# Where a two-layer hybrid encoder works off the conditioning weights of its first layer

## The chip, the cores and the metric

One core of one Trainium2 chip runs the whole program. The time is that of the device, from launch to end, in microseconds (us); lower is better. The engines are TensorE (PE; its weight loads are the row PEld), VectorE (DVE), ScalarE (ACT), GpSimd (POOL) and SyncE (SP), which here issues the loads.

## The reference

Two layers over x of 256 tokens by 1024 channels, float32. Each layer draws six vectors (shift, scale and gate, twice) from a conditioning vector c:

```python
c_act = jax.nn.silu(c)
for layer in range(DEPTH):
    ada = c_act @ ada_w[layer] + ada_b[layer]          # 1024 x 6144
    sh1, sc1, gt1, sh2, sc2, gt2 = jnp.split(ada, 6, axis=-1)
    h = modulate(rmsnorm(x, norm_mix_w[layer]), sh1, sc1)
    x = x + gt1[:, None, :] * token_mixer(h, positions, ...)
    h = modulate(rmsnorm(x, norm_ffn_w[layer]), sh2, sc2)
    f = swiglu(h, ...) if layer % 2 == 0 else moe_swiglu(h, ...)
    x = x + gt2[:, None, :] * f
return rmsnorm(x, final_norm_w)
```

The token mixer projects h to the inputs of a gated DeltaNet branch (short convolution, chunked delta rule with a triangular inverse per 64 tokens, then a scan over four chunks) and of a sliding-window attention branch, gates and merges both, and projects once more. The channel mixer is a dense SwiGLU (width 3584) in layer 0 and the top 2 of 8 experts in layer 1.

## The kernel before

**Units.** All weights come as units of 1 MB (128 partitions by 2048 float32) into a ring of six slots. The list `units`, written out by hand at the top, is the order of their loads and also the order in which VectorE takes them. SyncE issues the load of unit u once unit u - 6 is taken (`load`). Most units are split for TensorE: ScalarE copies them to `w_hi` in a rounded format, VectorE subtracts to get `w_lo` (`take`), and TensorE makes three products of high and low parts. Three pairs of `w_hi` and `w_lo` rotate. In ScalarE's and VectorE's programs `ahead(key, by)` works off all units up to that key and `by` split units more; `product` does that and then waits until TensorE has used the unit.

**Conditioning units.** `("ada", l, q, kh)` is half kh of the rows of 512 of the 6144 columns of `ada_w`; q runs from 0 to 11. They aren't split. VectorE adds four slices of 128x512, each times a column of silu(c), into `ada_acc` (L1687, L1689), and when both halves are in, TensorE sums over the partitions with small products against a column of ones, `ada_piece` (L1064), into four columns of a PSUM bank. `ada_columns` adds the bias. A third accumulation may not begin before TensorE has read the first of its buffer, so VectorE waits there for `ada_ps`. Of layer 0, q 0 to 3 (shift and scale of the mixer) are needed before its first projection, q 4 and 5 (its gate) and q 6 to 9 (shift and scale of the channel mixer) at the end of the token mixer, and q 10 and 11 (the last gate) only at the end of the channel mixer, where `gate_diag` and `gate_row` turn them into a row over all partitions.

**Order of layer 0's token mixer** (the same code runs for layer 1, without conditioning units, since those of layer 1 stand in layer 0's channel mixer). Split units: qkvz 0 to 5, swq 0 and 1, swkv, qkvz 6 and 7, gate 0 to 7, wb 0 and 1, wa 0 and 1, four mix. TensorE runs the projections, the attention, the intra-chunk products (last at L1295 on), half of gate 0, the first transposes of the inverse, then five levels of the inverse (`for lev in range(1, 6)`): products of L1321, the block of gate `lev`, products of L1345 and L1347. VectorE masks and subtracts between these, and takes gate `lev + 1` in between. Then come the scan over four chunks (from L1400) with pieces of gates 6 and 7 between its products, wb 0 and 1, wa 0 and 1, and the mix projection. wa needs `oa_lo`, which VectorE makes after it has read wb 0 and taken wa 0.

Conditioning units stand in the ring: three after qkvz 7, seven between the gates (taken ahead of level 1 and in levels 1 to 4: one, then 1, 1, 2, 2), two after each wb unit and two after wa 0. VectorE takes the first three at two `take_upto` calls between the softmax and the inverse. `ada_piece` stands after gate 0, in levels 1, 3, 4 and 5, after wb 0, after wb 1 and after wa 0.

**Layer 0's channel mixer** has 14 steps of fg, fu and the previous step's fd (`for i in range(2 * FC)`); two conditioning units of layer 1 and one `ada_piece` go with each of the steps 0 to 11. The router's slot numbers are made in bank 2 at step 1.

## Time and profile before

| | |
|---|---|
| median of 3 runs | 1880.84 us (1880.74 to 1880.88) |
| the profiled execution | 1880.96 us |
| its span, first to last instruction | 1879.2 us |
| TensorE busy | 96% of the span, granted clock 0.986 |
| VectorE busy | 80% |
| ScalarE busy | 56% |
| layer 0 token mixer | about 43 to 336 us |
| layer 0 channel mixer | about 336 to 601 us |
| layer 1 token mixer | about 601 to 866 us |
| experts | the rest |

Three kinds of rows are used. A row of the page gives an engine's busy time, share and number of instructions. A row of the timeline gives start and length in us, engine, line, operation, tiles, count, and in brackets how long the engine had been idle and what released it. A row of a stretch gives start:end and length, then busy time (and instructions) of PE, PEld, DVE, ACT and POOL, then the granted TensorE clock (1.00 is 2.4 GHz, 0.50 is 1.2 GHz), the mean share of the DMA engines, and GB/s. The ends of the stretches in layer 0's mixer are the starts of TensorE's instructions: 42.87 the first projection, 121.27 the attention's transposes, 153.69 the end of the intra-chunk products, 165.20 level 1 (L1321), 182.46, 194.32, 207.97 and 221.62 the gate blocks of levels 2 to 4 and what follows them, 232.76 the scan (L1400), 287.17 wa 0, 303.85 the mix projection. In layer 1 they are 601.16, 677.23, 709.63, 718.83, 732.97, 744.83, 756.69, 768.55, 778.86, 827.47 and 842.06. The step numbers of the channel mixer count from 0.

### The profile page before, as it was taken

The numbers are of one execution on the slowest core, as the hardware profiler recorded it, in microseconds if no ns is written. First come the engines' busy times: TensorE is split into PE (matmuls) and PEld (weight loads), VectorE is DVE, ScalarE is ACT, GpSimd is POOL, SyncE is SP. The second block draws the span as 40 slices with busy tenths as digits, with TensorE's granted clock in tenths as the row PEclk, the third lists the DMA queues.
The fourth block names the chain that finished last, engine by engine and source line by source line (L and its number), as shares of the span: only waits on it lengthen the run. The fifth ranks groups of instructions, "written<-read, shape, count | busy, mean of one in ns | idle before, by whom it ended". The sixth has DMA issues, their size and how long they took to land.

```text
span 1879.2 us, 26149 instructions
## 1 busy us (share of the span) xinstructions
PE 1799.1 (96%) x10008; PEld 1527.8 (81%) x10014; DVE 1498.2 (80%) x1449; ACT 1060.3 (56%) x903; POOL 72.2 (4%) x133
## 2 busy tenths in 40 slices
PE   6988999899999999989999999999999999999997
PEld 6878887899997879987778888888888888888875
DVE  6768748977765757456998898888988899888898
ACT  2453233433333462245667777777777777777765
POOL 4010000000000010000000001000000000000100
PEclk9999998999999999999999999999999999999999
DMA  8625636798873513235999999999999999999994
GB/s 299 197 90 181 200 113 224 244 318 297 281 261 108 161 58 106 74 113 179 345 335 367 387 352 387 371 358 389 359 375 369 363 390 359 368 383 353 388 392 172
DMA packets 261446, 519.94 MB, mean 277 GB/s; under 512 B 12170, under 2 KB 75892, under 8 KB 261364
## 3 DMA queue, kind: packets, MB, share of 16 engines
q1 hardware_dynamic: 257988, 506.21, 76.2%
q0 software_dynamic: 3376, 12.58, 1.7%
q8 instruction: 58, 0.95, 0.2%
q14 instruction: 24, 0.20, 0.0%
HBM read 510.90 MB, written 7.86 MB: 276 GB/s over the span
## 4 chain that ended last, share of the span: by engine, by line
PE 81%; DVE 13%; ACT 3%; issue 2%; DMA 1%; SPq 0%; DVEq 0%; ACTq 0%
PE bank L1043 18%; PE bank L1045 18%; PE bank L1044 18%; PE bank L1049 6%; PE bank L1051 5%; PE bank L1050 5%; DVE w_lo L1671 2%; DVE ada_acc L1689 2%; DVE w_lo L1791 1%; PE bank L1605 1%; ACT w_hi L729 1%; PE bank L1064 1%; PE bank L1347 1%; ACT w_hi L954 1%; DMA xs<-in_x_dram 1%
## 5 line engine op out<-in xcount | busy, mean ns | idle before, releaser
L1791 DVE TENSOR_TENSOR w_lo<-ring,w_hi 128x2048 fp32r<-128x2048 f32 x336 | 767.1, 2290 | 96.1 <-ACT w_hi L954 92.0
L954 ACT CAST w_hi<-ring 128x2048 fp32r<-128x2048 f32 x336 | 642.4, 1912 | 132.4 <-PE bank L1045 129.1
L1043 PE MATMUL bank<-w_hi,xg_hi 128*128 128x512 f32 x896 | 357.2, 399 | 0.7 <-DVE w_lo L1791 0.7
L1044 PE MATMUL bank<-w_lo,xg_hi 128*128 128x512 f32 x896 | 352.9, 394 | 0.0
L1045 PE MATMUL bank<-w_hi,xg_lo 128*128 128x512 f32 x896 | 352.9, 394 | 0.0
L1671 DVE TENSOR_TENSOR w_lo<-ring,w_hi 128x2048 fp32r<-128x2048 f32 x96 | 219.6, 2291 | 99.1 <-ACT w_hi L729 98.5
L1049 PE MATMUL bank<-hT_hi,w_hi 128*128 128x256 f32 x912 | 265.5, 291 | 12.1 <-DVE w_lo L1671 8.1
L1050 PE MATMUL bank<-hT_lo,w_hi 128*128 128x256 f32 x912 | 258.4, 283 | 0.0
L1051 PE MATMUL bank<-hT_hi,w_lo 128*128 128x256 f32 x912 | 258.3, 283 | 0.0
L729 ACT CAST w_hi<-ring 128x2048 fp32r<-128x2048 f32 x96 | 182.3, 1903 | 79.6 <-PE bank L1045 42.1
L1043 PEld LDWEIGHTS bank<-w_hi,xg_hi 128*128 128x128 f32 x896 | 168.1, 188 | 42.7 <-issue 2.7
L1045 PEld LDWEIGHTS bank<-w_hi,xg_lo 128*128 128x128 f32 x896 | 168.0, 188 | 40.5
L1044 PEld LDWEIGHTS bank<-w_lo,xg_hi 128*128 128x128 f32 x896 | 168.1, 188 | 38.1
L1049 PEld LDWEIGHTS bank<-hT_hi,w_hi 128*128 128x128 f32 x912 | 174.9, 192 | 18.4 <-issue 7.8
L1043 PE MATMUL bank<-w_hi,h_hi 128*128 128x512 f32 x448 | 180.8, 404 | 0.0
L1050 PEld LDWEIGHTS bank<-hT_lo,w_hi 128*128 128x128 f32 x912 | 175.3, 192 | 1.5 <-issue 1.4
L1045 PE MATMUL bank<-w_hi,h_lo 128*128 128x512 f32 x448 | 176.2, 393 | 0.0
L1044 PE MATMUL bank<-w_lo,h_hi 128*128 128x512 f32 x448 | 175.7, 392 | 0.0
L1051 PEld LDWEIGHTS bank<-hT_hi,w_lo 128*128 128x128 f32 x912 | 175.2, 192 | 0.0
L1689 DVE SCALAR_TENSOR_TENSOR ada_acc<-ring,c_silu,ada_acc 128x512 f32<-128x512 f32 x160 | 120.2, 751 | 5.7
L1045 PEld LDWEIGHTS bank<-w_hi,h_lo 128*128 128x128 f32 x448 | 84.0, 188 | 20.1
L1044 PEld LDWEIGHTS bank<-w_lo,h_hi 128*128 128x128 f32 x448 | 84.3, 188 | 17.6
(417 smaller groups left out, 2158.7 us busy)
## 6 DMA issues: line engine op xcount, KB each, us to landing
ring<-in_moe_w_gate_dram SPq DMA_DIRECT2D x112, 1024.0 KB, 7.3
ring<-in_moe_w_up_dram SPq DMA_DIRECT2D x112, 1024.0 KB, 7.5
ring<-in_moe_w_down_dram SPq DMA_DIRECT2D x112, 1024.0 KB, 7.3
ring<-in_ada_w_dram SPq DMA_DIRECT2D x48, 1024.0 KB, 5.5
ring<-in_w_in_dram SPq DMA_DIRECT2D x38, 1024.0 KB, 5.2
ring<-in_ffn_w_gate_dram SPq DMA_DIRECT2D x14, 1024.0 KB, 7.0
ring<-in_ffn_w_up_dram SPq DMA_DIRECT2D x14, 1024.0 KB, 5.1
ring<-in_ffn_w_down_dram SPq DMA_DIRECT2D x14, 1024.0 KB, 6.5
```

The costliest lines, as they stand in the source:

```text
L729: act.copy(w_hi[buf][:], ring[:, ring_slot, :]).then_inc(hi_ready, 1)
L954: act.copy(w_hi[MOE_BUF[p % NS_MOE]][:], ring[:, p % RING, :]).then_inc(hi_ready, 1)
L1043: pe.matmul(o, xh, wh, start=start, stop=False)
L1044: pe.matmul(o, xh, wl, start=False, stop=False)
L1045: return pe.matmul(o, xl, wh, start=False, stop=stop)
L1049: pe.matmul(o, wh, xh, start=start, stop=False)
L1050: pe.matmul(o, wh, xl, start=False, stop=False)
L1051: return pe.matmul(o, wl, xh, start=False, stop=stop)
L1064: ins = pe.matmul(ps[bank][:, 4 * q + c:4 * q + c + 1], ada_acc[:, (NQ * l + q) % 2, c * P:(c + 1) * P], ones[:, 0:1], start=not begun, st ...
L1671: dve.tensor_tensor(w_lo[buf_of[s]][:], ring[:, u % RING, :], f32(w_hi[buf_of[s]][:]), ALU.subtract).then_inc(taken, 1)
L1689: ins = dve.scalar_tensor_tensor(acc, w[:, kk, :], ck, acc, ALU.mult, ALU.add)
L1791: dve.tensor_tensor(w_lo[b][:], ring[:, p % RING, :], f32(w_hi[b][:]), ALU.subtract).then_inc(taken, 1)
```

## The change

Of layer 0's sixteen conditioning units q 4 to 11, twelve stay in the token mixer and four (q 10, 11) move to steps 0 and 1 of the channel mixer; layer 1's then stand in steps 2 to 13. In the ring, q 4 goes between swq 1 and swkv, the first half of q 5 between swkv and qkvz 6, one unit after each of the gates 1 to 5, q 8 after gate 7, and q 9 after wa 0. VectorE's two extra `take_upto` calls go. `ada_piece` stands after gate 0 as before, then in levels 2 and 4, after wb 0, after wb 1 and after wa 1. In the channel mixer the columns of q 10 and 11 go to bank 2, so the router's slot numbers there move by 128 columns; the gate diagonal is made at step 2 instead of 12, layer 1's columns are read after the last step, and the gate row uses bank 0 instead of 3, with a wait for the last SiLU. The warming matmuls at the start of layer 1 write to bank 1.

```diff
--- before.py
+++ after.py
@@ -72,19 +72,19 @@
             units.append((("qkvz", l, j), True))
         for kh in range(2):
             units.append((("swq", l, kh), True))
+        if l == 0:
+            ada_units(2)
         units.append((("swkv", l), True))
+        if l == 0:
+            ada_units(1)
         for j in (6, 7):
             units.append((("qkvz", l, j), True))
-        if l == 0:
-            ada_units(3)
         for j in range(8):
             units.append((("gate", l, j), True))
             if l == 0:
-                ada_units((1, 1, 1, 2, 2, 0, 0, 0)[j])
+                ada_units((0, 1, 1, 1, 1, 1, 0, 2)[j])
         for cc in range(2):
             units.append((("wb", l, cc), True))
-            if l == 0:
-                ada_units(2)
         for cc in range(2):
             units.append((("wa", l, cc), True))
             if l == 0 and cc == 0:
@@ -94,7 +94,7 @@
                 units.append((("mix", l, cc, kh), True))
 
     mixer_units(0)
-    ada1 = [("ada", 1, q, kh) for q in range(NQ) for kh in range(2)]
+    ada1 = ada0 + [("ada", 1, q, kh) for q in range(NQ) for kh in range(2)]
     for i in range(2 * FC):
         units.append((("fg", i), True))
         if ada1:
@@ -1152,7 +1152,7 @@
                             turn_x(0, m_xn)
                         ada_piece(0, q, 0, True)
                 else:
-                    warm(24, 0)
+                    warm(24, 1)
                     turn_x(2 * l, m_xn)
                 def narrow(w, bank):
 
@@ -1323,8 +1323,8 @@
                         ins.then_inc(u_ps, 1)
                     pe.wait_ge(gate_s, 8 * l + lev)
                     two_blocks(("gate", l, lev), 0)
-                    if l == 0 and lev != 2:
-                        ada_piece(0, {1: 5, 3: 6, 4: 7, 5: 8}[lev], 1)
+                    if l == 0 and lev in (2, 4):
+                        ada_piece(0, 4 + lev // 2, 1)
                     if lev == 5:
 
                         pe.wait_ge(kgb_s, l + 1)
@@ -1434,19 +1434,19 @@
                 pe.wait_ge(gate_s, 8 * (l + 1))
                 half_branch("wb", 0, (2, 3), ob_hi, ob_lo, 1)
                 if l == 0:
-                    ada_piece(0, 9, 1)
+                    ada_piece(0, 7, 1)
                 half_branch("wb", 1, (0, 5), ob_hi, ob_lo, 0)
                 pe.wait_ge(ln2_s, 2 * (l + 1))
                 half_branch("wb", 1, (0, 5), ob_hi, ob_lo, 1)
                 if l == 0:
-                    ada_piece(0, 10, 1)
+                    ada_piece(0, 8, 1)
                 pe.wait_ge(oa_s, l + 1)
                 branch("wa", 0, (6, 7), oa_hi, oa_lo)
-                if l == 0:
-                    ada_piece(0, 11, 1)
                 half_branch("wa", 1, (4, 5), oa_hi, oa_lo, 0)
                 pe.wait_ge(yb_s, 4 * l + 2)
                 half_branch("wa", 1, (4, 5), oa_hi, oa_lo, 1)
+                if l == 0:
+                    ada_piece(0, 9, 1)
                 for kh in range(2):
                     pe.wait_ge(y_s, 2 * l + kh + 1)
                     for cc in range(2):
@@ -1493,14 +1493,17 @@
                         two_blocks(("fu", i), 1)
                         if i:
                             f_down(i - 1)
-                        if i < NQ:
-                            ada_piece(1, i, 3)
+                        if i < 2:
+                            ada_piece(0, NQ - 2 + i, 2)
+                        else:
+                            ada_piece(1, i - 2, 3)
                         if i == 1:
                             pe.wait_ge(upper_s, 1)
-                            pe.matmul(ps[2][:, 0:P], ones[:], upper[:], start=True, stop=True)
-                            pe.matmul(ps[2][:, P:P + 2], upper[:], ones[:, 0:2], start=True,
+                            pe.matmul(ps[2][:, P:2 * P], ones[:], upper[:], start=True, stop=True)
+                            pe.matmul(ps[2][:, 2 * P:2 * P + 2], upper[:], ones[:, 0:2], start=True,
                                       stop=True).then_inc(logit_ps, 1)
-                    gate_row(2, f_dg, (2, 3))
+                    pe.wait_ge(fs_s, 2 * FC)
+                    gate_row(2, f_dg, (2, 0))
                     f_down(2 * FC - 1)
 
 
@@ -1908,11 +1911,7 @@
                     dve.tensor_tensor(KB[:, :, here], kT[:, :, here], beta, ALU.mult)
                     dve.tensor_tensor(vT[:, :, here], vT[:, :, here], beta, ALU.mult).then_inc(kb_s, 1)
                 divide(1)
-                if l == 0:
-                    take_upto(u_of[("ada", 0, 4, 0)])
                 out_low(0)
-                if l == 0:
-                    take_upto(u_of[("ada", 0, 5, 0)])
 
                 dve.wait_ge(exps_s, 6 * l + 6)
                 link(dve.tensor_tensor(XT, X, wide(before_blk[:], [P, TB * H, P], 1), ALU.mult))
@@ -2024,7 +2023,7 @@
                     dve.tensor_tensor(hT_lo[:, half, :], y_sum[:, half, :], f32(hT_hi[:, half, :]),
                                       ALU.subtract).then_inc(y_s, 1)
                 if l == 0:
-                    ada_columns(0, 1, NQA, NQ)
+                    ada_columns(0, 1, NQA, NQ - 2)
                     dve.wait_ge(ada_s, 2)
                 gate_diag(2 * l + 1, l, 2, m_dg)
                 ahead(("mix", l, 1, 1), 0)
@@ -2074,18 +2073,19 @@
                         dve.tensor_tensor(f_lo[i % 2][:], f_h[:], f32(f_hi[i % 2][:]), ALU.subtract).then_inc(fhl_s, 1)
                         if i == 2:
                             dve.wait_ge(logit_ps, 1)
-                            dve.tensor_copy(slots[:], ps[2][:, 0:P])
+                            dve.tensor_copy(slots[:], ps[2][:, P:2 * P])
                             for tb in range(TB):
-                                dve.tensor_scalar(tok_c[:, tb, 0:1], ps[2][:, P:P + 1], float(tb * P), None, ALU.add)
-                            dve.tensor_scalar(spare, ps[2][:, P:P + 1], float(2 * T), None, ALU.add)
-                            dve.tensor_scalar(spare_n, ps[2][:, P:P + 1], -1.0, -float(2 * T), ALU.mult, ALU.add)
-                            link(dve.tensor_scalar(rsm[:, 0, :], ps[2][:, 0:E], -1.0, float(E), ALU.mult, ALU.add))
-                        if i == NQ:
-                            ada_columns(1, 3, 0, NQ)
+                                dve.tensor_scalar(tok_c[:, tb, 0:1], ps[2][:, 2 * P:2 * P + 1], float(tb * P), None, ALU.add)
+                            dve.tensor_scalar(spare, ps[2][:, 2 * P:2 * P + 1], float(2 * T), None, ALU.add)
+                            dve.tensor_scalar(spare_n, ps[2][:, 2 * P:2 * P + 1], -1.0, -float(2 * T), ALU.mult, ALU.add)
+                            link(dve.tensor_scalar(rsm[:, 0, :], ps[2][:, P:P + E], -1.0, float(E), ALU.mult, ALU.add))
+                            ada_columns(0, 2, NQ - 2, NQ)
                             dve.wait_ge(ada_s, 3)
                             gate_diag(2, 0, 5, f_dg[:])
+                    ada_columns(1, 3, 0, NQ)
+                    dve.wait_ge(ada_s, 4)
                     ahead(("fd", 2 * FC - 1), 0)
-                    gate_copy(2, f_gt, (2, 3))
+                    gate_copy(2, f_gt, (2, 0))
                     for tb in range(TB):
                         if tb == 0:
                             dve.wait_ge(first_ps, 2)
```

## Rows read from the trace of the kernel before

**Rows 1.** The page: busy time of each engine.
```profile
PE 1799.1 (96%) x10008; PEld 1527.8 (81%) x10014; DVE 1498.2 (80%) x1449; ACT 1060.3 (56%) x903; POOL 72.2 (4%) x133
```

**Rows 2.** Stretches of layer 0's mixer: start:end, length, each engine's busy time, clock.
```profile
42.87:121.27 78.40, 74.90 (x506) 67.59 (x507) 50.00 (x90) 40.11 (x48) 4.95 (x6) 0.98 0.58 188
...
153.69:165.20 11.51, 9.06 (x66) 9.05 (x65) 10.61 (x14) 0.89 (x3) 0.00 (x0) 0.85 0.37 120
165.20:182.46 17.26, 14.29 (x123) 13.94 (x122) 13.52 (x16) 4.16 (x3) 0.00 (x0) 1.00 0.71 243
182.46:194.32 11.86, 11.37 (x99) 11.18 (x98) 10.20 (x13) 2.38 (x2) 0.00 (x0) 1.00 0.55 178
194.32:207.97 13.65, 12.52 (x107) 12.14 (x106) 12.77 (x16) 2.39 (x2) 0.00 (x0) 1.00 0.68 194
...
221.62:232.76 11.14, 10.37 (x91) 10.18 (x89) 4.27 (x4) 4.43 (x6) 0.00 (x0) 1.00 0.50 141
232.76:287.17 54.41, 48.40 (x351) 43.76 (x352) 30.29 (x38) 17.95 (x21) 0.00 (x0) 0.94 0.39 128
287.17:303.85 16.68, 15.63 (x105) 15.54 (x106) 14.77 (x16) 2.94 (x2) 0.00 (x0) 0.79 0.86 304
```

**Rows 3.** The same stretches in layer 1's mixer, cut at the same instructions.
```profile
601.16:677.23 76.07, 72.58 (x507) 65.24 (x507) 47.90 (x78) 39.90 (x46) 4.95 (x6) 0.98 0.44 139
...
709.63:718.83 9.20, 6.88 (x56) 6.68 (x56) 8.97 (x13) 0.96 (x3) 0.00 (x0) 1.00 0.37 114
718.83:732.97 14.14, 13.41 (x112) 13.06 (x113) 8.72 (x9) 4.08 (x3) 0.00 (x0) 1.00 0.58 149
732.97:744.83 11.86, 11.38 (x99) 11.19 (x98) 7.29 (x9) 2.38 (x2) 0.00 (x0) 1.00 0.39 90
...
768.55:778.86 10.31, 9.53 (x84) 9.34 (x82) 4.27 (x4) 4.28 (x6) 0.00 (x0) 1.00 0.30 102
778.86:827.47 48.61, 43.95 (x335) 39.68 (x335) 19.06 (x22) 17.87 (x21) 0.00 (x0) 0.99 0.20 66
827.47:842.06 14.59, 14.29 (x96) 14.09 (x96) 9.25 (x9) 3.17 (x3) 0.00 (x0) 0.79 0.47 146
```

**Rows 4.** VectorE in order of time: one pair of conditioning units and the next split.
```profile
265.76 0.49 DVE L1687 TENSOR_SCALAR ada_acc<-ring,c_silu 128x512 f32<-128x512 f32 x1 [0.56 <-ACT work L899]
...
271.74 2.29 DVE L1671 TENSOR_TENSOR w_lo<-ring,w_hi 128x2048 fp32r<-128x2048 f32 x1
```

**Rows 5.** VectorE and then TensorE in order of time, around swkv in layer 0.
```profile
93.64 4.50 DVE L1671 TENSOR_TENSOR w_lo<-ring,w_hi 128x2048 fp32r<-128x2048 f32 x2 [2.50 <-ACT w_hi L729]
106.25 2.29 DVE L1671 TENSOR_TENSOR w_lo<-ring,w_hi 128x2048 fp32r<-128x2048 f32 x1 [8.11 <-ACT w_hi L729]
...
103.60 0.69 PE L1043 MATMUL bank<-w_hi,hT_hi 128*128 128x256 f32 x1
```

**Rows 6.** Layer 1's mixer: VectorE in order of time, and a wait of TensorE.
```profile
740.79 0.69 DVE L1963 TENSOR_TENSOR work<-work,bank 128x512 f32<-128x512 f32 x1 [3.42 <-PE bank L1347]
...
809.01 2.29 DVE L1671 TENSOR_TENSOR w_lo<-ring,w_hi 128x2048 fp32r<-128x2048 f32 x1 [8.12 <-ACT w_hi L729]
...
828.53 2.28 DVE L1671 TENSOR_TENSOR w_lo<-ring,w_hi 128x2048 fp32r<-128x2048 f32 x1
...
PE bank L1049 <- DVE oa_lo L2012: 4.5, 1, 4.5
```

**Rows 7.** Two stretches at the start of the channel mixer, columns as in rows 2.
```profile
342.22:344.87 2.65, 0.00 (x0) 0.00 (x0) 2.65 (x3) 2.62 (x4) 0.00 (x0) 1.00 0.42 70
345.40:348.80 3.40, 3.40 (x18) 3.40 (x18) 3.29 (x5) 1.04 (x1) 0.00 (x0) 0.50 1.04 389
```

**Rows 8.** Channel mixer steps 11 and 12 as stretches; VectorE in step 3.
```profile
531.24:549.10 17.86, 17.86 (x129) 16.75 (x128) 12.64 (x10) 6.73 (x5) 0.00 (x0) 1.00 0.84 295
549.91:566.95 17.04, 17.04 (x122) 15.95 (x122) 9.21 (x7) 6.17 (x5) 0.00 (x0) 1.00 0.60 186
...
397.71 2.29 DVE L1671 TENSOR_TENSOR w_lo<-ring,w_hi 128x2048 fp32r<-128x2048 f32 x1 [1.79 <-ACT w_hi L729]
```

## The prediction

> **What bounds the kernel now.** I read the page first: TensorE is busy 96% of the span, VectorE 80% [rows 1], so as a whole the kernel is a TensorE kernel, and only a stretch in which TensorE waits or runs slowly can give anything back. A "unit" here is one 1 MB piece of weights; conditioning units are worked off by VectorE alone (four multiply-adds of 128x512), all others are split by ScalarE and VectorE for TensorE. The two token mixers are the same code; only the first carries conditioning units: 16 in its ring order. So I cut both mixers at the same TensorE instructions and laid the lengths side by side [rows 2, 3]. That is the view that decides. The query/key/value part differs by 2.3 us (78.40 and 76.07), all of it in the first matmuls, ahead of what the change touches. From the end of the intra-chunk products on, layer 0 is longer by 2.31 us (start of the inverse), 3.12, 0, 1.79, 1.79 and 0.83 (levels 1 to 5), 5.80 (scan to the start of the last branch) and 2.09 (last branch): 17.7 us in all, the most that conditioning can cost there. Level 2, with one unit and no column product, costs nothing: 11.86 in both layers, as in levels 3 and 4 of layer 1 (level 4 of layer 0 is like its level 3). So a unit costs nothing while VectorE has idle time in front of what it must deliver; in levels 3 and 4, with two units each, it has not.
>
> **Prices.** A pair of units takes VectorE 271.74 - 265.76 = 5.98 us, about 2.9 and 3.1 for its halves [rows 4]. The column product that TensorE makes of each finished pair costs 11.14 - 10.31 = 0.83 us (level 5, the only difference there [rows 2, 3]).
>
> **The change part by part,** in order of time. My model of layer 0 after is layer 1 before plus the units and products that it still has.
>
> 1. Three units go ahead of the key/value weights: two between the last query unit and "swkv", one behind it. VectorE splits the last query unit and swkv back to back, 4.50 us from 93.64, so the second starts near 95.85 [rows 5]. With the pair between, swkv's low part is ready at 95.85 + 5.98 + 2.29 = 104.12. TensorE wants it at 103.60 [rows 5]. What is queued behind: VectorE's next split, which has 8.11 us of idle time before it [rows 5] and takes the third unit for nothing, and ScalarE's copies of swkv's result, on which the whole normalisation chain hangs, so the delay is not absorbed. Cost +0.56 (0.5 to 1.0). The weights behind are loaded three places later in the six-slot ring: the load of qkvz 7 is issued when swq 1 is taken, near 95.9, and its split comes after that of 106.25, over 10 us later, against 3.6 us of transfer for 1 MB at 295 GB/s [rows 8]; it hides.
>
> 2. The three units between softmax and the inverse vanish. Layer 0 goes from 11.51 to layer 1's 9.20 [rows 2, 3]; its one column product (unchanged, q 4) falls into the wait for VectorE that layer 1 has there. I take 9.27: -2.24. Much of that is clock: it was 0.85 here against 1.00 in layer 1 [rows 2, 3], which is half speed for 0.3 x 11.51 = 3.45 us and costs up to half of that, 1.7. If the clock falls all the same, the gain is only 0.5.
>
> 3. Levels 1 to 5 carry 1, 1, 1, 1, 1 units instead of 1, 1, 2, 2, 0, the one ahead of level 1 goes, and products come at levels 2 and 4 instead of 1, 3, 4 and 5. The least idle time of VectorE in a layer 1 level is 3.42 us [rows 6] against at most 3.1 for a unit, so all five hide, by 0.3 us or more. Level 1: 17.26 to 14.14, -3.12. Level 2: 11.86 to 11.86 + 0.83, +0.83. Level 3: 13.65 to 11.86, -1.79. Level 4: 13.65 to 12.69, -0.96. Level 5: 11.14 to 10.31, -0.83. Sum -5.87. Were the 0.3 us not there, each level would lose up to 0.5.
>
> 4. The last pair of the scan (q 8) stands before the first branch weights: VectorE is idle 8.12 us there in layer 1 [rows 6], enough for 5.98. The pairs that stood ahead of the second "wb" unit, the first "wa" unit and so on (6 us each, in front of oa_lo, for which TensorE waits) go. In layer 1 TensorE still waits 4.5 us for oa_lo [rows 6], and the products of q 7 and q 8 (1.7 us) fall into that. So 54.41 becomes 48.61: -5.80 (the largest term).
>
> 5. Last branch. The pair q 9 now stands before the second "wa" unit. In layer 1's times its split runs at 828.53 [rows 6]; with the pair, it is ready at 828.53 + 5.98 + 2.29 = 836.8, 9.3 us after the branch begins at 827.47. Then the second half unit takes TensorE 5.8 us at full clock and the product 0.8: 15.9 after 16.68 before. But half of such a unit falls in a slow stretch in both layers (granted clock 0.79 [rows 2, 3]), and the wait ahead of the unit invites another, worth up to 1.7 us (half of 3.4). I take 17.3: +0.6, with -0.8 and +1.0 as ends. Output projection and norm are unchanged; what is late next there is TensorE itself.
>
> 6. Channel mixer. The four units stand where two of layer 1's pairs stood, and everything shifts by two steps; only steps 12 and 13 gain load. The gate diagonal and a column copy move on VectorE from step 12 to step 2: a pass over half the elements of a split (half of 2.25 [rows 5]) and a copy of 8 columns, some 1.4 us, within its 1.79 us of idle time before the next split that waits [rows 8]. DMA share rises in step 12 from 0.60 towards 0.84, as in step 11, where TensorE was busy 17.86 of 17.86 us [rows 8]. What does cost is TensorE: two more products in a stretch where it never rests: +1.66. The extra wait before the gate row (the SiLU of the last step) is long met, one f_down earlier; the bank numbers cost nothing.
>
> **Sum:** +0.56 - 2.24 - 5.87 - 5.80 + 0.6 + 1.66 = -11.1 us. The profiled execution was 1880.96 us (span 1879.2), the median of the runs 1880.84, so I apply it to the median as it stands: 1880.84 - 11.1 = 1869.7.
>
> **The clock, trace against page.** TensorE waited 2.65 us at 342.22 and the granted clock then stood at 0.50 (1.2 GHz) for 3.4 us [rows 7]. The Trainium skill (TensorE: Matmul & The Clock Gate, "HAM oscillation") lets only idle gaps longer than this one re-throttle the array; the trace disagrees. By the page, the shorter gaps of part 2 could never have lowered the clock, and its 1.7 us would not be there to gain: the sum would be 9.4. By the row a wait of such a length can bring half speed behind it. Everything after layer 0's mixer shifts by some 11 us, so that slow stretches of layer 1 may come or go, up to 1.7 us each.
>
> **Rivals.**
> A. *Half the gain.* VectorE's chain is not what sets the inverse, scan and branch; with the units gone ScalarE or the clock holds the same events, so the middle of the stages keeps. Priced as parts 2, 4 and 5 at half: -1.1 - 5.87 - 2.9 + 1.0 + 0.56 + 1.66 = -6.7, 1874.2. Against it: layer 1 runs the same chain in the short time on the same engines. Chance 0.13.
> B. *More.* Part 5 keeps the clock (-0.8 instead of +0.6) and two of layer 1's slow stretches vanish. Half speed for 3.4 us holds 18 matmuls [rows 7]; at full speed step 12 ran 122 in 17.04, 24 in that time [rows 8]: 0.9 us lost, at most 1.7, so 1.3 each: -11.1 - 1.4 - 2.6 = -15.1, 1865.7. Chance 0.13.
> C. *Slower: the load queue.* The channel mixer is the stretch with the highest DMA share, 0.84 [rows 8]. If the 4 MB moved there can't be hidden, they cost their transfer, 4.2 MB at 295 GB/s = 14.2 us, against 11.1 gained plus nothing: +3.1, 1884. It decides once less than 3 us of these transfers find room. Against it: step 12 moved 186 GB/s for 17.04 us, so room for two more units is there [rows 8]. Chance 0.02.
> D. *The change does little:* pair q 4 ahead of swkv is late by its load, and the chain of part 1 loses what the inverse gains: within 0.2% (3.8 us). It needs swkv some 8 us late, where my sum has it half a microsecond late. Chance 0.02.
>
> **How the numbers follow.** The forecast holds with 0.70 (1867.5 to 1872). The 80% range takes in the forecast, B and the near part of A: 1865.5 to 1873.5. A measurement of this kernel can tell about 0.2% (3.8 us) from no change; forecast, B and most of A are beyond it: faster 0.95, same 0.03, slower 0.02.
>
> **What would show it.** In the changed trace: swkv's first matmul waits about half a microsecond for w_lo; the inverse start takes 9.3 us at granted clock 1.00; the levels take 14.1, 12.7, 11.9, 12.7, 10.3; the scan stage 48.6 with TensorE still waiting near 3 us for oa_lo; TensorE waits for w_lo before the second wa unit; channel mixer steps 12 and 13 at 17.9 us each. Wrong would be: a level over 13 us, a wait on a DMA in the channel mixer, or an oa_lo wait over 4 us.

## The result, and the profile after

The changed kernel takes 1867.24 us (median) against 1880.74 for the kernel before in the same session: a ratio of 0.9928 [0.9908, 0.9947], 13.5 us less. One of its five executions is slow (2629.68 us at a granted clock of 0.628); the other four took 1862.07 to 1870.31 us, with a median of 1865.9. The profiled one took 1867.24 us, with a span of 1865.5. Measured twice more, on two other chips, its median was 1866.91 and 1867.41 (ratios 0.9933 and 0.9941, below).

On the page of the changed kernel, in the line that answers to [rows 1], VectorE has the same 1498 us of work; TensorE is busy for 1789.0 us and not 1799.1, with as many products as before (two fewer in the token mixer, two more in the channel mixer), since less of its work ran slowly. What changed is where the work stands. Next the stretches of layer 0, cut at the same TensorE instructions as [rows 2] (start:end, length, busy time and instructions of PE, PEld, DVE, ACT and POOL, granted TensorE clock, DMA share, GB/s):

```profile
42.02:120.28 78.26, 73.07 (x507) 65.90 (x507) 58.19 (x102) 40.11 (x48) 4.95 (x6) 0.97 0.70 229
120.28:151.46 31.18, 27.62 (x175) 19.99 (x173) 24.09 (x35) 23.35 (x58) 0.00 (x0) 1.00 0.00 1
151.46:160.68 9.22, 7.62 (x66) 7.58 (x65) 8.99 (x13) 0.98 (x3) 0.00 (x0) 1.00 0.36 116
160.68:174.81 14.13, 13.40 (x113) 13.05 (x113) 11.63 (x13) 4.06 (x3) 0.00 (x0) 1.00 0.69 221
174.81:187.57 12.76, 12.28 (x108) 12.09 (x106) 9.94 (x13) 2.38 (x2) 0.00 (x0) 1.00 0.51 168
187.57:199.42 11.85, 11.37 (x99) 11.17 (x98) 10.11 (x12) 2.38 (x2) 0.00 (x0) 1.00 0.53 178
199.42:212.17 12.75, 12.27 (x108) 12.07 (x106) 9.85 (x12) 2.38 (x2) 0.00 (x0) 1.00 0.62 164
212.17:222.47 10.30, 9.52 (x83) 9.33 (x81) 7.18 (x8) 4.27 (x6) 0.00 (x0) 1.00 0.48 111
222.47:271.10 48.63, 45.64 (x351) 41.49 (x351) 24.81 (x30) 17.97 (x21) 0.00 (x0) 1.00 0.40 130
271.10:288.59 17.49, 15.58 (x105) 15.38 (x105) 15.30 (x17) 3.50 (x3) 0.00 (x0) 0.80 0.82 285
...
321.02:587.79 266.77, 261.49 (x1840) 241.34 (x1841) 207.08 (x216) 101.97 (x82) 0.00 (x0) 0.99 0.80 276
```

Read it row by row beside [rows 2]: the inverse start is 9.22 (was 11.51), the five levels are 14.13, 12.76, 11.85, 12.75 and 10.30 (were 17.26, 11.86, 13.65, 13.65, 11.14), the scan 48.63 (was 54.41), the last branch 17.49 (was 16.68). VectorE's column says why: in each level it now is busy for 7 to 12 us of 10 to 14, where in the two levels with two units it was busy 12.77 of 13.65. The channel mixer is 266.77 against 264.95 before:

```profile
336.21:601.16 264.95, 259.61 (x1823) 239.54 (x1825) 196.01 (x199) 101.97 (x82) 0.00 (x0) 0.99 0.77 263
```

What TensorE waited for in layer 0's mixer tells the same. Waits of TensorE (engine, line, what it waited for: us in total, times, longest), first before, from 42 to 345 us:

```profile
PE bank L1064 <- DVE ada_acc L1689: 3.1, 2, 2.5
PE bank L1321 <- DVE work L1965: 3.1, 4, 1.1
...
PE bank L1043 <- DVE w_lo L1671: 2.2, 1, 2.2
PE bank L1049 <- DVE oa_lo L2012: 1.5, 1, 1.5
```

and then of the changed kernel, same bounds:

```profile
PE bank L1043 <- DVE w_lo L1674: 3.8, 2, 2.2
PE bank L1049 <- DVE oa_lo L2011: 2.8, 1, 2.8
PE bank L1321 <- DVE work L1964: 1.9, 4, 0.5
```

The waits for a finished conditioning pair (`ada_acc`, 3.1 us) are gone, those for masked blocks (`work` at the level's L1321) fell from 3.1 to 1.9, which is the same as in layer 1. Two waits grew. L1043 (2.2 to 3.8) has a new one of 1.68 us for swkv's low part, behind the pair that now stands ahead of it. The one for `oa_lo` grew from 1.5 to 2.8 because TensorE no longer waits on the way there.

The scan is the largest gain, and its granted clock rose as well (0.94 to 1.00). What sets its end is VectorE. Before, VectorE had no gap from 265.76 [rows 4] to the end of `oa_lo` at 287.12, and TensorE, which had waited 1.5 us for it, went on at 287.17:

```profile
278.23 5.55 DVE L1689 SCALAR_TENSOR_TENSOR ada_acc<-ring,c_silu,ada_acc 128x512 f32<-128x512 f32 x7
283.70 2.28 DVE L1671 TENSOR_TENSOR w_lo<-ring,w_hi 128x2048 fp32r<-128x2048 f32 x1
285.90 1.22 DVE L2012 TENSOR_TENSOR oa_lo<-work,oa_hi 128x1024 fp32r<-128x1024 f32 x1
```

In the changed kernel it has nothing to do for 2.92 us ahead of wa 0's split, until ScalarE's copy is there:

```profile
267.62 2.29 DVE L1674 TENSOR_TENSOR w_lo<-ring,w_hi 128x2048 fp32r<-128x2048 f32 x1 [2.92 <-ACT w_hi L729]
269.83 1.22 DVE L2011 TENSOR_TENSOR oa_lo<-work,oa_hi 128x1024 fp32r<-128x1024 f32 x1
```

Term by term, with lengths from the two profiled executions:

| | forecast | measured |
|---|---|---|
| 1 query/key/value part | +0.56 | -0.14 |
| 2 start of the inverse | -2.24 | -2.29 |
| 3 five levels | -5.87 | -5.77 |
| 4 scan | -5.80 | -5.78 |
| 5 last branch | +0.6 | +0.81 |
| 6 channel mixer | +1.66 | +1.82 |
| sum of the terms | -11.1 | -11.35 |
| start, before the first projection | none | -0.85 (42.87 to 42.02) |
| attention of layer 0 | none | -1.24 (32.42 to 31.18) |
| layer 1's mixer, as a whole | none | -1.93 (264.42 to 262.49) |
| experts | none | +1.57 (1005.17 to 1006.74) |
| the rest | none | +0.10 |
| span | -11.1 | -13.7 (1879.2 to 1865.5) |

The lower block is TensorE's clock. The attention is the plainest of these: 32.42 at 0.95 became 31.18 at 1.00, and layer 1's attention, in which nothing was changed, is 32.35 at 0.95 in this run and 31.19 at 1.00 in others. In layer 1's mixer it is the query/key/value part, 76.07 at 0.98 and 74.45 at 1.00. The start can't be read from the column, which has 1.00 before and 0.93 after. Early in the kernel before, the column doesn't show TensorE's pace: the first 25 matmuls of the projection follow each other every 0.21 us and the next ones every 0.12 us, all at a granted clock of 1.00. By that pace the start did get faster: its last 16 column products of L1076 took 3.55 us before and 1.93 after.

### The profile page after: what moved, and what is told of

Same layout as the page of the kernel before. It is cut to its first block, busy times and chain, and to the rows that moved or that the text cites. A ratio compares the mean times of both kernels' runs of the same rounds, so it can differ in the third digit from the quotient of the medians.

```text
span 1865.5 us, 26158 instructions
## 1 busy us (share of the span) xinstructions
PE 1789.0 (96%) x10014; PEld 1518.7 (81%) x10014; DVE 1497.6 (80%) x1450; ACT 1060.0 (57%) x903; POOL 71.0 (4%) x133
## 3 DMA queue, kind: packets, MB, share of 16 engines
HBM read 510.90 MB, written 7.86 MB: 278 GB/s over the span
## 4 chain that ended last, share of the span: by engine, by line
PE 81%; DVE 11%; ACT 4%; issue 2%; DMA 1%; SPq 0%; DVEq 0%; ACTq 0%
PE bank L1043 18%; PE bank L1045 18%; PE bank L1044 18%; PE bank L1049 6%; PE bank L1051 5%; PE bank L1050 5%; DVE w_lo L1674 2%; DVE w_lo L1794 1%; PE bank L1608 1%; ACT w_hi L729 1%; PE bank L1347 1%; DVE ada_acc L1692 1%; PE bank L1064 1%; DMA ring<-in_w_in_dram 1%; PE bank L1345 1%
## 5 line engine op out<-in xcount | busy, mean ns | idle before, releaser
L1043 PE MATMUL bank<-w_hi,xg_hi 128*128 128x512 f32 x896 | 357.2, 399 | 0.7 <-DVE w_lo L1794 0.7
L1043 PEld LDWEIGHTS bank<-w_hi,xg_hi 128*128 128x128 f32 x896 | 168.1, 188 | 42.9 <-issue 2.8
L1043 PE MATMUL bank<-w_hi,h_hi 128*128 128x512 f32 x448 | 180.8, 404 | 0.0
```

The costliest lines, as they stand in the source:

```text
L1043: pe.matmul(o, xh, wh, start=start, stop=False)
```

## The experiments

Each was timed against the kernel before on its own chip. The edits are against the changed kernel unless said otherwise. Ratios are to the kernel before, with 95% intervals.

### The change again, twice

> The changed kernel unaltered, on another chip and with another profile. Its first profile was 13.7 us below the kernel before and 2.5 us below the forecast, and its single times lay between 1862 and 1870 us. Theory (work is fixed, only TensorE's half-speed stretches move): the stages of layer 0's mixer from the inverse to the last branch repeat within 0.1 us (9.2, 14.1, 12.8, 11.9, 12.8, 10.3, 48.6), and what differs between this profile and the first one sits in stretches with another granted clock. Rival (waits differ from run to run): the lengths of the levels and of the scan differ by over 0.5 us at granted clock 1.00.

> The changed kernel unaltered once more, as the reference for the two variants beside it on the same chip. Theory: 1864 to 1869 us, scan stage 48.6 and levels 14.1, 12.8, 11.9, 12.8, 10.3 for the fourth time; its profile differs from the others only in where half speed falls. Rival: a stage at full speed differs by over 0.5 us.

Measured: 1866.91, ratio 0.9933 [0.9918, 0.9947], and 1867.41, ratio 0.9941 [0.9924, 0.9957]. These two give the spread to read all else against: the profiled executions had spans of 1863.3 and 1859.9 us, though the code is the same. The stage lengths say where the difference lies. The last branch of layer 0, then the channel mixer, in the second of the two:

```profile
271.20:287.17 15.97, 14.06 (x104) 13.86 (x105) 15.30 (x17) 3.51 (x3) 0.00 (x0) 0.89 0.78 276
...
319.62:584.90 265.28, 259.92 (x1839) 239.83 (x1841) 206.98 (x216) 101.86 (x82) 0.00 (x0) 1.00 0.81 278
```

Against 17.49 at 0.80 and 266.77 at 0.99 above: 1.5 us each, and only the clock column differs. The inverse start, the five levels and the scan, all at clock 1.00, had the same length within 0.02 us in the three executions; the inverse start, for one, 9.22, 9.21 and 9.21. So the rival (waits that differ from run to run) is out.

### Only the last gate moved

The ring, the products and VectorE's two extra calls as before; q 10 and 11 in the channel mixer.

```diff
-        if l == 0:
-            ada_units(2)
         units.append((("swkv", l), True))
-        if l == 0:
-            ada_units(1)
         for j in (6, 7):
             units.append((("qkvz", l, j), True))
+        if l == 0:
+            ada_units(3)
...
-                ada_units((0, 1, 1, 1, 1, 1, 0, 2)[j])
+                ada_units((1, 1, 1, 2, 2, 0, 0, 0)[j])
...
+            if l == 0 and cc == 0:
+                ada_units(2)
         for cc in range(2):
             units.append((("wa", l, cc), True))
-            if l == 0 and cc == 0:
-                ada_units(2)
...
```

> One part alone: only the four units of q 10 and 11 go to the channel mixer, all others stand as in the kernel before. Theory (VectorE's order decides, worked out by VectorE's program): inverse start and levels stay as before (11.5, 17.3, 11.9, 13.6, 13.6, 11.1); the scan stage falls by 3 us from 54.4, because the pair of q 9 still stands before the second wb unit; the last branch falls from 16.7 to 14.4; the channel mixer grows by 1.7. In all -3.6 us against before. Rival (the move is the whole gain): -11 us or more, with shorter levels too.

Measured: 1876.52, ratio 0.9987 [0.9976, 0.9998]: 2.9 us gained. Its stretches from the start of the inverse to the last branch:

```profile
150.37:160.44 10.07, 7.61 (x64) 7.59 (x64) 9.84 (x13) 0.96 (x3) 0.00 (x0) 1.00 0.42 135
160.44:181.02 20.58, 16.83 (x121) 16.48 (x121) 14.28 (x17) 4.08 (x3) 0.00 (x0) 0.83 0.61 204
...
231.31:282.76 51.45, 46.79 (x344) 42.24 (x344) 24.71 (x30) 17.94 (x21) 0.00 (x0) 0.97 0.30 103
282.76:296.19 13.43, 13.13 (x96) 12.93 (x97) 9.24 (x9) 3.17 (x3) 0.00 (x0) 0.87 0.49 159
```

With one pair instead of two ahead of `oa_lo`, the scan is 51.45, half way from 54.41 to 48.63; with none ahead of wa 1, the last branch is 13.43. But level 1 took 20.58 instead of 17.26, which no moved unit explains and which was expected to stay. TensorE's wait for gate 1's low part, and a stretch behind it with its clock:

```profile
165.76 0.55 PE L1047 MATMUL bank<-hT_hi,w_hi 128*128 128x256 f32 x1 [3.27 <-DVE w_lo L1668]
```

```profile
167.40:170.80 3.40, 3.40 (x17) 3.40 (x17) 3.33 (x4) 0.00 (x0) 0.00 (x0) 0.50 0.98 339
```

In the kernel before the same wait was 2.49 us (169.71), with the clock at 1.00 for all of level 1 [rows 2]. In this run the inverse start ran at 1.00 and not at 0.85, so that TensorE came sooner, waited 3.27 us for the same VectorE chain (the unit that stands ahead of gate 1), and ran at half speed for about 6.8 us. Of the 3.3 us, 0.8 are the longer wait and 2.5 are slower matmuls (TensorE busy 16.83 and not 14.29). So the unit ahead of level 1 is the one that costs most: 3.1 by VectorE, and 2.5 more when the clock falls with it.

### Only the spreading

All sixteen conditioning units stay; q 8 and 9 before the wb units, q 10 and 11 as the pairs before wa 0 and wa 1.

```diff
         for cc in range(2):
             units.append((("wb", l, cc), True))
+            if l == 0:
+                ada_units(2)
...
-    ada1 = ada0 + [("ada", 1, q, kh) for q in range(NQ) for kh in range(2)]
+    ada1 = [("ada", 1, q, kh) for q in range(NQ) for kh in range(2)]
...
```

> The other part alone: q 4 to 8 spread as in the change, but all sixteen units stay in the token mixer (q 9 after wb 0, q 10 after wb 1, q 11 after wa 0; column products of q 7 at level 5, q 8 and 9 after the wb units, q 10 and 11 after the wa units). Theory: inverse start 9.2, levels 14.1, 12.8, 11.9, 12.8, 11.1, scan stage unchanged at 54.4, last branch 17 to 18, channel mixer unchanged at 265.0: -6.5 us against before. With the other part the two add up to about the whole (-10 to -13). Rival (DMA or ScalarE holds the levels once all units stay): levels over 13 us and less than half of it.

Measured: 1873.59, ratio 0.9968 [0.9956, 0.998]: 5.8 us gained. Its first stretch and its scan:

```profile
42.37:119.94 77.57, 72.39 (x507) 65.22 (x508) 58.21 (x102) 40.13 (x48) 4.95 (x6) 1.00 0.71 231
...
223.01:277.43 54.42, 48.56 (x352) 44.33 (x352) 36.04 (x46) 17.94 (x21) 0.00 (x0) 0.94 0.53 167
```

The scan is 54.42, as before the change (54.41), though it now also holds q 8's pair: that one is free, in front of wb 0, and the two behind it cost what they cost before. The inverse start and levels 1 to 4 are as in the changed kernel; level 5 is 11.16 and not 10.30, since it holds the product of q 7. So parts 2 and 3 come from the spreading, but for level 5, and part 4 needs four units fewer ahead of `oa_lo`. The channel mixer, untouched in this run, took 266.18 and not the 265.0 expected: 6.8 us at half speed follow its wait for fu 0, and 3.4 in the kernel before.

The two halves give 2.9 and 5.8 us, the whole 12.5 to 13.5. The stretches from inverse start to last branch say where the rest is: these are 150.16 us before, 145.82 with the gate alone (-4.3), 143.77 with the spreading alone (-6.4), 137.13 with both (-13.0). So 2.3 us of the difference lie in these stretches. The 3.3 us of level 1 with the gate alone are more than that; without them the halves would come to -14.0, 1 us over the whole. The rest lies outside these stretches and is not assigned here.

### The key/value weights ahead of the pair

```diff
-        if l == 0:
-            ada_units(2)
         units.append((("swkv", l), True))
-        if l == 0:
-            ada_units(1)
         for j in (6, 7):
+            if l == 0:
+                ada_units(8 - j)
             units.append((("qkvz", l, j), True))
```

> The change with one part undone: the pair of q 4 stands behind swkv, where VectorE is idle 8.1 us, and the first half of q 5 between qkvz 6 and 7. Theory (the pair in front of swkv delays TensorE): the wait of 1.7 us ahead of swkv's first matmul is gone, the query stage is 1.7 us shorter than in the change, all else equal: -1.7 us, or -0.6 if TensorE runs the unit before at half speed. Rival (ScalarE's copies set the chain behind it anyway): the wait goes, but the attention starts as late as before, 0.

Measured: 1864.55, ratio 0.9915 [0.9898, 0.9932], beside 0.9933 [0.9918, 0.9947] of the changed kernel on the same chip: 2.4 us less at the median, with intervals that overlap, so the gain isn't shown by the whole time. First the changed kernel around swkv, VectorE and then TensorE:

```profile
92.31 2.29 DVE L1674 TENSOR_TENSOR w_lo<-ring,w_hi 128x2048 fp32r<-128x2048 f32 x1 [2.50 <-ACT w_hi L729]
94.52 0.48 DVE L1690 TENSOR_SCALAR ada_acc<-ring,c_silu 128x512 f32<-128x512 f32 x1
95.03 5.54 DVE L1692 SCALAR_TENSOR_TENSOR ada_acc<-ring,c_silu,ada_acc 128x512 f32<-128x512 f32 x7
100.49 2.29 DVE L1674 TENSOR_TENSOR w_lo<-ring,w_hi 128x2048 fp32r<-128x2048 f32 x1
...
102.93 0.36 PE L1043 MATMUL bank<-w_hi,hT_hi 128*128 128x256 f32 x1 [1.68 <-DVE w_lo L1674]
```

and VectorE with the key/value weights first (the pair stands between the two lines):

```profile
92.56 4.50 DVE L1672 TENSOR_TENSOR w_lo<-ring,w_hi 128x2048 fp32r<-128x2048 f32 x2 [2.50 <-ACT w_hi L727]
...
105.10 2.29 DVE L1672 TENSOR_TENSOR w_lo<-ring,w_hi 128x2048 fp32r<-128x2048 f32 x1 [2.06 <-ACT w_hi L727]
```

The pair fits behind swkv with 2.06 us to spare, and TensorE's wait of 1.68 us is gone. In this profile the first stretch is no shorter for it, 78.08 at clock 0.95 beside 78.26 at 0.97: the wait of 2.16 us ahead of the last query unit was followed by half speed here and not in the changed kernel. The price of part 1 is best read where the clock is out of it: the first stretch was 77.57 with the pair ahead of swkv (the spreading alone) and 75.63 without (the gate alone), both at clock 1.00. That is 1.9 us, not 0.56.

### The last pair ahead of wa 0

```diff
         for cc in range(2):
             units.append((("wb", l, cc), True))
+            if l == 0 and cc == 1:
+                ada_units(2)
         for cc in range(2):
             units.append((("wa", l, cc), True))
-            if l == 0 and cc == 0:
-                ada_units(2)
```

> The change with the pair of q 9 one place earlier, before wa 0 instead of wa 1, so that it stands in front of oa_lo. Theory (the scan stage fell because 6 us of units left the chain wb 0 read, wa 0 split, oa_lo): the stage grows by 3 us from 48.6 to about 51.7, since ScalarE's path to wa 0 hides the other 3; the last branch falls by 2.9 or more to 14 to 15. Near 0 in the whole time. Rival (VectorE isn't what TensorE waits for there): scan stage stays at 48.6, the whole falls by 3 us.

Measured: 1866.89, ratio 0.9929 [0.9914, 0.9945], the same as the changed kernel. Scan and last branch:

```profile
224.64:276.23 51.59, 45.64 (x352) 41.49 (x352) 30.38 (x38) 18.00 (x21) 0.00 (x0) 0.97 0.49 156
276.23:290.33 14.10, 14.10 (x105) 14.10 (x105) 9.60 (x9) 3.53 (x3) 0.00 (x0) 0.85 0.55 186
```

The wait for `oa_lo` is 5.8 us instead of 2.8, the one for wa 1 is 0.2 instead of 1.9. 65.69 together, against 48.63 + 17.49 = 66.12 or 48.63 + 15.97 = 64.60 in the changed kernel. The pair costs about 3 us ahead of wa 0, where 2.92 of its 6 us of VectorE find idle time. Ahead of wa 1 it costs 1.9 us (15.97 - 14.10), or 3.4 with a half-speed stretch. Neither place has room for all of it.

### Each column product of the channel mixer twice

```diff
-                for c in range(4):
+                for c in (0, 1, 2, 3, 0, 1, 2, 3) if again else range(4):
...
-                            ada_piece(1, i - 2, 3)
+                            ada_piece(1, i - 2, 3, again=True)
```

(and so for q 10 and 11; the second product writes the same values over the first).

> The change with the column products of the channel mixer's 14 steps issued twice; the second writes the same columns again. Theory (TensorE never rests there, so every product is paid in full, 0.83 us each): the channel mixer grows by 14 x 0.83 = 11.6 us, the whole too. Rival (products hide in TensorE's queue beside weight loads or in waits for VectorE): growth under 6 us.

Measured: 1879.29, ratio 0.9993 [0.998, 1.0006], which is 0.0052 to 0.0065, or 9.8 to 12.2 us, above the three ratios of the changed kernel. The channel mixer:

```profile
322.84:601.89 279.05, 273.76 (x1952) 253.61 (x1953) 207.12 (x216) 101.85 (x82) 0.00 (x0) 0.99 0.77 264
```

279.05 - 266.77 = 12.28 us for 14 products: 0.88 each, paid in full. TensorE hardly rests there and hides nothing, so part 6 is two products and no more: 1.75 of the 1.82 measured.

### Filling TensorE's wait for `oa_lo`

Ten matmuls on a constant, into a free bank, ahead of the wait, in both layers.

```diff
+                warm(10, 6)
                 pe.wait_ge(oa_s, l + 1)
                 branch("wa", 0, (6, 7), oa_hi, oa_lo)
```

> The change with ten warming matmuls of 128x512 (2.2 us at full speed) on TensorE in front of its wait for oa_lo, in both layers; they fill the idle time and delay nothing. Theory (the idle time there is what brings TensorE to half speed in the branch behind it): the granted clock of the last branch rises from about 0.8 to 1.00; the branch of layer 1 falls from 14.0 or more to under 12.5, that of layer 0 by 1 us or more; the whole by 2 to 4 us. Rival (the clock falls for another reason, or the branch is held by VectorE): no change in either stage; or the scan stage grows because the matmuls run late.

Measured: 1864.65, ratio 0.992 [0.9906, 0.9934], an interval that overlaps those of the changed kernel; both stages missed what was expected. In layer 0 the wait of 2.8 us became 0.6 and the branch began at clock 1.00, but it is as long as ever, 17.49. Cut where its second unit begins, first with the filling:

```profile
270.90:280.29 9.39, 5.96 (x49) 5.76 (x49) 9.07 (x12) 1.90 (x1) 0.00 (x0) 1.00 0.79 250
280.29:288.39 8.10, 8.10 (x56) 8.10 (x57) 6.22 (x6) 1.60 (x2) 0.00 (x0) 0.79 0.94 325
```

and the changed kernel, then its first repetition:

```profile
271.10:280.48 9.38, 7.47 (x49) 7.27 (x49) 9.06 (x12) 1.82 (x1) 0.00 (x0) 0.82 0.73 253
280.48:288.59 8.11, 8.11 (x57) 8.11 (x57) 6.24 (x6) 1.68 (x3) 0.00 (x0) 0.79 0.93 323
```

```profile
280.50:287.09 6.59, 6.59 (x57) 6.59 (x57) 6.24 (x6) 1.68 (x3) 0.00 (x0) 1.00 0.89 307
```

The first part is 9.4 us at either clock: TensorE ran the first unit faster and then waited 3.4 us instead of 1.9 for wa 1's low part, which stands behind the pair. VectorE (busy 9.1 of 9.4) sets it. The second part is TensorE's own, 8.1 us when the clock falls at its start and 6.6 when not. In layer 1 ten matmuls left 2.33 us of the wait of 4.5:

```profile
813.64 0.39 PE L1049 MATMUL bank<-oa_hi,w_hi 128*128 128x256 f32 x1 [2.33 <-DVE oa_lo L2012]
```

and the clock fell all the same: 0.55 over the 3.36 us behind it, with 17 matmuls. Layer 1's scan and last branch were 50.19 and 13.44, as in the changed kernel's second repetition without filling (50.18 and 13.44).

### Another order at the start of the channel mixer

In step 0 both conditioning units stand behind fu 0; the later steps keep their order.

```diff
         units.append((("fg", i), True))
-        if ada1:
+        if i:
             units.append((ada1.pop(0), False))
         units.append((("fu", i), True))
-        if ada1:
+        if not i:
             units.append((ada1.pop(0), False))
+        units.append((ada1.pop(0), False))
```

> The change with the first pair of units of the channel mixer behind fu 0 instead of around it. Theory (the 2.7 us that TensorE waits for fu 0 in step 0 are VectorE's first half unit, and half speed follows the wait): the wait goes, so does the slow stretch behind it, step 0 gets shorter by 2.7 to 4.2 us and the whole as much. Rival (fg 1 and the units behind are late instead): the wait moves to fg 1 and nothing or at most 1 us is gained.

Measured: 1867.12, ratio 0.993 [0.9916, 0.9944], no gain; the idea that the order costs the wait at fu 0 fell. VectorE has the same work ahead of step 1, and the wait came in pieces. TensorE in order of time:

```profile
329.74 0.39 PE L1050 MATMUL bank<-hT_hi,w_hi 128*128 128x256 f32 x1 [1.12 <-DVE w_lo L1675]
338.01 0.36 PE L1050 MATMUL bank<-hT_hi,w_hi 128*128 128x256 f32 x1 [1.24 <-DVE w_lo L1675]
```

1.12 and 1.24 here and 0.49 later, 2.85 us in three, where the changed kernel has 2.67 in one. No half speed followed, and the channel mixer took 266.06; with the single wait it took 266.77 at clock 0.99 and 265.28 at 1.00.

### No conditioning unit before wa 1, and then the waits filled too

The key/value weights first, as above. q 5's second half goes between softmax and inverse, where the kernel before had two calls; the levels carry one unit each with three products; the last three units stand behind gate 7, and VectorE takes the first of them in the scan's second chunk. The second kernel also has 10 warming matmuls before wa 0 in layer 0 and 19 in layer 1.

```diff
-                ada_units((0, 1, 1, 1, 1, 1, 0, 2)[j])
+                ada_units((0, 1, 1, 1, 1, 1, 0, 3)[j])
...
-            if l == 0 and cc == 0:
-                ada_units(2)
...
+                        if l == 0 and n == 1:
+                            take_upto(u_of[("ada", 0, 8, 1)])
...
+                warm((10, 19)[l], 6)
                 pe.wait_ge(oa_s, l + 1)
```

> The change with every unit moved to a place where VectorE is idle in layer 1: q 4 behind swkv and the first half of q 5 behind qkvz 6 (as in the third experiment), its second half behind the first out_low, q 6 to the first half of q 8 in the five levels, the second half of q 8 inside the scan, q 9 after gate 7; column product of q 7 at level 5, of q 8 and 9 before the wait for oa_lo. Theory (a unit costs nothing exactly where VectorE has idle time ahead of its next deadline): query stage -1.7, level 5 +0.8, scan stage 48.6, last branch from 16 to 17.5 down to 13.4 to 14.4: -4 us against the change, 1863. Rival (the clock takes back what the waits give, as when swkv's wait went): the stages fall as said at full speed, but the whole by under 1.5 us. Other rival: the unit inside the scan delays the state by 0.5 us or more.

> The variant beside it, with warming matmuls sized to fill all of TensorE's wait for oa_lo: 10 in layer 0, 19 in layer 1 (4.2 us of the 4.5). Ten in each had left 2.3 us of the wait in layer 1 and half speed had come all the same. Theory (idle TensorE time brings half speed): with the wait filled layer 1's scan stage and last branch run at granted clock 1.00 and together take 48.6 + 12 = 60.6 instead of 62.5 to 63.6. Rival (something else than idle time, such as the narrow matmuls of the scan or norms, brings half speed there): together 62.5 or more and granted clock under 0.95.

Measured: 1864.54, ratio 0.9924 [0.9908, 0.994], and 1858.76, ratio 0.9893 [0.9879, 0.9908]; the changed kernel had 0.9941 [0.9924, 0.9957] on the same chip. The first is 2.9 us under it at the median where 4 were expected, with intervals that overlap. The second is the best kernel of this study: 21 us under the kernel before and about 8.7 under the change, with an interval clear of the latter's. Its scan and last branch in layer 0, then the last branch in layer 1:

```profile
221.50:270.13 48.63, 47.75 (x361) 42.32 (x362) 27.82 (x34) 17.84 (x21) 0.00 (x0) 1.00 0.48 147
270.13:282.05 11.92, 11.62 (x96) 11.42 (x96) 9.24 (x9) 3.18 (x3) 0.00 (x0) 1.00 0.55 178
...
805.75:817.67 11.92, 11.62 (x96) 11.41 (x97) 9.25 (x9) 3.17 (x3) 0.00 (x0) 1.00 0.56 179
```

The scan still holds three conditioning units and is still 48.63: they are free there. The branch is 11.92 in both layers, at clock 1.00. In the first of the two kernels, without the filling, it is 13.38 at 0.88 and 13.44 at 0.87. So of the branch's 17.49 us in the changed kernel, 4.1 are the pair with its wait, its product (0.85, now ahead of the wait for `oa_lo`) and a half-speed stretch, and 1.5 the half speed that the `oa_lo` wait brings. In layer 1, scan and last branch together are 60.55 us with the wait filled, and 62.05 to 63.63 in the profiles of all other runs, before and after: this gain is the filling's. Another 3 us of this profile are not: the experts took 1003.54 at clock 1.00 and 1006.73 at 0.99 in the first of the two, but 1003.50 also in one execution of the changed kernel. With 0.6 and 0.4 us of the waits left, the clock didn't fall behind them; with 2.3 left it did.

## Why the prediction came out right

The time (1867.2) is in the range and on the right side, 2.5 us below the forecast of 1869.7. The mechanism is the one that was forecast; that the terms add up so closely is in part luck (step 1, and what the sum left out). By its steps:

**The view that decides** was right. The two mixers are the same code, and layer 0 without its load did become layer 1 plus products. The five levels came within 0.07 us each; the inverse start within 0.05; the scan 48.63 against 48.61. The assumption in steps 3 and 4 that a unit is free while VectorE has over 3 us of idle time in front of what it must deliver held in all five levels, with 0.48 us of VectorE's idle time left in the tightest (level 3); so rival A (the same events held by ScalarE or the clock) is out. Its price had halved parts 2 and 4 but kept part 3 whole, which its own words don't allow. The half-and-half runs agree: the scan's gain is 2.9 us for each pair taken from ahead of `oa_lo` (54.41, 51.45, 48.63), as step 4 had it with -5.80 for two. The step didn't say that a pair takes 6 us of VectorE and is worth only half of that there; the other half stands in VectorE's wait for ScalarE's copy of wa 0, shown above.

**Step 1 was right on the numbers it read, and mis-sized as a price.** Its own terms give 104.12 - 103.60 = +0.52, where it wrote +0.56. From the last query unit's split to swkv's first matmul it was 103.60 - 93.64 = 9.96 us before and 102.93 - 92.31 = 10.62 after, +0.66 for a forecast of +0.56. But those rows of before carry a half-speed stretch: its last query unit ran from 95.98 with the granted clock at 0.60 over the first 3.5 us:

```profile
95.50:99.00 3.50, 3.02 (x8) 2.34 (x9) 2.64 (x2) 0.32 (x1) 0.00 (x0) 0.60 0.54 152
```

At full speed TensorE wants swkv 1.6 us sooner: with the gate alone it began 8.37 us after that split (100.29 - 91.92). So the wait is 1.68 us, not the half that the text gave, and the stretch pays 1.9. It is net -0.14 by luck: that half-speed stretch is gone (the rest of the part is +0.34), and the first matmuls, up to L1161, took 7.86 us and not 8.34. A slack measured behind a slow stretch is not a slack that one may count on.

**Step 2** was right in size; its reason (most of it clock) is shown only in part. Without the two early calls the stretch is 9.22 at 1.00. With them and the clock at 1.00 (the gate alone) it is 10.07. So of the 2.3 us gained, 0.85 are VectorE's and 1.44 the clock, within the 1.7 that the text allowed.

**Step 5** took 17.3 and got 17.49, with 15.97 in two other executions, inside its ends. Its parts are exact: the second unit was to be ready 9.3 us after the start of the branch and was after 9.38; unit and product were to take 5.8 + 0.8 = 6.6 and took 6.59 at full speed, 8.11 when the clock fell. The clock stayed a matter of chance, as the text had it, at 1.5 where the text allowed 1.7.

**Step 6** was low by 0.16: the product costs 0.88 in the channel mixer where 0.83 was read from level 5. No transfer was late; the last steps ran as the text wanted them, 17.9 us each:

```profile
533.93:551.79 17.86, 17.86 (x130) 16.75 (x128) 13.65 (x14) 6.73 (x5) 0.00 (x0) 1.00 0.83 294
551.79:569.66 17.87, 17.87 (x130) 16.76 (x129) 10.47 (x9) 4.92 (x4) 0.00 (x0) 1.00 0.93 294
```

TensorE is busy without a gap beside DMA shares of 0.83 and 0.93, so rival C (the queue) is out, and so is D.

**What the sum left out** is the lower block of the table: net 2.4 us of half speed that went away, most of it in stretches that the change doesn't touch. The text had it as a rival (B, two stretches of layer 1 vanishing, 2.6), and about that much happened, if not all in layer 1 and with one more in the experts. It is not settled whether the change causes it: three profiled executions of the same code had spans of 1865.5, 1863.3 and 1859.9, with the differences in stretches of another granted clock, so all of the 2.4 can be chance of one run. The medians (-13.5, -12.5 and -12.7 against the kernel before) are steadier and leave 1 to 2 us beyond the sum, whose cause stays open.

**The clock rule weighed in the prediction.** Half speed followed waits of 2.16 us (the kernel before, and the key/value weights first), 2.33 (layer 1 with ten matmuls), 2.67 (the changed kernel) and 3.27 us (the gate alone). The Trainium skill (TensorE: Matmul & The Clock Gate, "HAM oscillation") lets only gaps longer than any of these lower the clock. The trace disagrees, and the sum of 9.4 that followed from that rule was further off than 11.1.

## What to carry to other kernels

Where the same code runs twice and only one of the two carries an extra load, lay both out in stretches cut at the same instructions: the lighter one is the forecast for the heavier once its load is spread, and here it held to 0.1 us in the inverse start, the levels and the scan. Spread such a load one unit to each place where its engine idles longer than the unit takes, keep it off the chain that a matmul waits for, and count what is paid on the saturated engine (the product) in full. Measure slack only where the clock was high. If a wait ahead of a dense stretch is to be filled, fill it nearly whole: the one partial filling that left over 2 us gained nothing.

## What the runs showed of the hardware

The same wait doesn't always bring half speed. The changed kernel and its first repetition both wait for fu 0's low part, 2.67 and 2.68 us, at a clock of 1.00. The 3.41 us behind it, changed kernel first:

```profile
329.69:333.10 3.41, 3.41 (x16) 3.41 (x17) 3.30 (x5) 1.57 (x1) 0.00 (x0) 0.51 1.00 390
```

```profile
328.22:331.63 3.41, 3.41 (x28) 3.41 (x29) 3.30 (x5) 1.58 (x1) 0.00 (x0) 1.00 1.05 389
```

16 matmuls in one and 28 in the other, in the same 3.41 us and with the same work on VectorE, ScalarE and DMA. The wait of 2.16 us ahead of the last query unit is another such case: half speed before, full speed in the changed kernel. What decides between them isn't visible in these rows. It goes with what moves this kernel by some 10 us from one execution to the next (1861.65 us at a mean clock of 0.992, 1872.1 at 0.987 in one session), while the inverse start, the levels and the scan at full clock repeat within 0.02 us. So a forecast made from one profile can hardly be better than a few us here, and a comparison of stages is sharper than one of totals.
